# Hybrid decoder step on one core: the norm of k moved into the projection, tokens loaded and turned ahead, first weights rounded between modulated tiles

## What is computed

```python
m = silu(c) @ w_ada + b_ada             # shift1, scale1, gate1, shift2, scale2, gate2
h = x * (1 + scale1) + shift1
proj = h @ w_in                         # r, k, v, decay, a, gate columns, then q and kv latents and the rotary key
z = p_rwkv + mu * (shifted - p_rwkv)    # token shift; new_shift is the last row of p_rwkv
a = sigmoid(a0 + ad @ a2); g = sigmoid(gd) @ g2
kk = heads(k * k_k)
kk = kk / maximum(sqrt(sum(kk * kk, -1, keepdims=True)), 1e-12)
S, o = wkv_scan(S0, r, decay, k * (1 + (a - 1) * k_a), v, kk, a)
q = rmsnorm(cq, q_norm) @ w_q_up; lat = rmsnorm(ckv, kv_norm); kr = rope(kr, pos)
```

## Time and profile before

| | us |
|---|---|
| median of 3 runs | 2091.32 |
| lowest and highest run | 2089.89 and 2097.28 |
| profiled execution, its own time | 2096.06 |
| its span (first to last instruction) | 2094.3 |
| PE busy | 1862.8 (89%) |
| DVE busy | 1226.0 (59%) |
| POOL, ACT busy | 387.1, 381.1 (18% each) |

### The profile page before, as it was taken

One profiled execution on the slowest core, in us unless ns is written; L12 is line 12 of the kernel. 1 busy time (PEld: TensorE's weight loads), 2 busy tenths in 40 slices (PEclk: granted clock), 3 DMA queues, 4 the chain that ended last, 5 costly groups with the idle time before them and its releaser, 6 DMA issues.

```text
span 2094.3 us, 36235 instructions
## 1 busy us (share of the span) xinstructions
PE 1862.8 (89%) x14280; PEld 1637.6 (78%) x14280; DVE 1226.0 (59%) x1880; ACT 381.1 (18%) x809; POOL 387.1 (18%) x543
## 2 busy tenths in 40 slices
PE   5899996799999898773789599998999999989995
PEld 2688994577777665552579589998999999989995
DVE  1345854765666373230367777665766676657766
ACT  0433334223223232120210130000000000000002
POOL 0000102233333134523001341000100010001113
PEclk8899998899999896596999789999999999999997
DMA  9598521566666524105065325554555555545531
GB/s 350 192 333 311 168 86 48 167 213 215 209 217 196 182 76 119 49 20 183 1 201 161 121 83 167 170 166 141 161 161 161 158 166 162 161 128 169 168 100 45
DMA packets 300692, 329.08 MB, mean 157 GB/s; under 512 B 30419, under 2 KB 268532, under 8 KB 300084
## 3 DMA queue, kind: packets, MB, share of 16 engines
q1 hardware_dynamic: 291394, 314.83, 46.4%
q10 hardware_dynamic: 5548, 8.21, 1.2%
q0 software_dynamic: 3584, 3.68, 0.6%
HBM read 321.47 MB, written 5.21 MB: 156 GB/s over the span
## 4 chain that ended last, share of the span: by engine, by line
PE 82%; DVE 6%; DMA 5%; issue 3%; ACT 2%; SPq 1%; POOL 0%; ACTq 0%; DVEq 0%
PE bank L1347 15%; PE bank L1349 15%; PE bank L1348 15%; PE bank L1370 3%; DMA slab<-in_w_ada_dram 3%; PE bank L1371 3%; PE bank L1372 3%; PE bank L1484 3%; PE bank L1546 2%; PE bank L1556 2%; PE bank L1879 2%; PE bank L1554 1%; PE bank L1857 1%; PE bank L1332 1%; DVE xT L2505 1%
## 5 line engine op out<-in xcount | busy, mean ns | idle before, releaser
L1347 PE MATMUL bank<-arena_hi 128*128 128x288 f32 x2304 | 692.1, 300 | 32.9 <-DVE hT_lo L2049 19.7
L1349 PE MATMUL bank<-arena_hi,slab_lo 128*128 128x288 f32 x2304 | 684.6, 297 | 0.0
L1347 PEld LDWEIGHTS bank<-arena_hi 128*128 128x128 f32 x2304 | 438.1, 190 | 40.1 <-DVE hT_lo L2049 25.0
L1349 PEld LDWEIGHTS bank<-arena_hi,slab_lo 128*128 128x128 f32 x2304 | 440.8, 191 | 13.8 <-issue 13.8
L1348 PE MATMUL bank<-hT_lo,arena_hi 128*128 128x288 f32 x1280 | 384.8, 301 | 13.5 <-issue 13.5
L2445 DVE TENSOR_TENSOR slab_lo<-slab,arena_hi 128x2048 fp32r<-128x2048 f32 x144 | 352.1, 2445 | 5.0
L2444 DVE CAST arena_hi<-slab 128x2048 fp32r<-128x2048 f32 x144 | 176.8, 1228 | 302.3 <-PE bank L1349 294.9
L1348 PE MATMUL bank<-arena_hi 128*128 128x288 f32 x1024 | 302.1, 295 | 0.0
L1348 PEld LDWEIGHTS bank<-hT_lo,arena_hi 128*128 128x128 f32 x1280 | 247.5, 193 | 0.0
L1348 PEld LDWEIGHTS bank<-arena_hi 128*128 128x128 f32 x1024 | 192.2, 188 | 0.0
L878 POOL TENSOR_TENSOR arena<-arena 128x288 f32<-128x288 f32 x64 | 68.3, 1067 | 669.6 <-ACT arena L1275 669.6
(11 more groups left out here) (403 smaller groups left out, 2494.8 us busy)
## 6 DMA issues: line engine op xcount, KB each, us to landing
slab<-in_w_ada_dram SPq DMA_DIRECT2D x64, 1024.0 KB, 5.5
slab<-in_w_up_dram SPq DMA_DIRECT2D x32, 2048.0 KB, 8.8
slab<-in_w_down_dram SPq DMA_DIRECT2D x32, 2048.0 KB, 8.6
slab<-in_w_ada_dram SPq DMA_DIRECT2D x16, 2048.0 KB, 13.5
slab<-in_w_in_dram SPq DMA_DIRECT2D x15, 2048.0 KB, 11.4
slab<-in_w_out_dram SPq DMA_DIRECT2D x8, 2048.0 KB, 9.1
slab<-in_cache_latent_dram SPq DMA_DIRECT2D x96, 128.0 KB, 2.4
slab<-in_cache_latent_dram ACTq DMA_DIRECT2D x32, 128.0 KB, 3.5
```

The source lines that it names most:

```text
L1347: pe.matmul(b[0:w, 0:NTOK], w_hi[:, k, 0:w], x_hi[:, k, :], start=(k == 0), stop=False)
L1349: mm = pe.matmul(b[0:w, 0:NTOK], w_lo[:, k, 0:w], x_hi[:, k, :], start=False, stop=(k == KT - 1))
```

## The change

Three things.

- **Norm of k inside the projection.** While the projection runs, ACT squares k * k_k (parts 44 to 47 and 52 to 55), PE sums the squares of four tiles at a time into four 32-partition groups of one bank (`kk_sums`), ACT takes the square roots of two whole banks, and DVE takes maximum and reciprocal of both tiles in two instructions. In the LoRA loop a small product (`kk_spread`) spreads the two rows of a head tile over its 128 partitions, and DVE makes k * k_k * 1/norm in one instruction. POOL's products, the eight square roots and the eight reciprocals go. The last rows are turned by plain products into 32-partition groups of banks 4 and 5, after parts 57 and 59, copied by DVE between later weights and stored in 14 DMAs that SP issues ahead of the LoRA weights. tanh and sigmoid of the LoRA inputs move into the projection. The latents' norm and the key's rotation move to the four chunk steps of the last head tile. Some scratch tiles get other places.
- **Tokens ahead.** x is loaded by SP ahead of the first slabs. PE turns tokens 0 to 7 ahead of half 0, 8 to 11 ahead of half 1 and 12 to 15 behind turn 0, into four banks by turns.
- **First weights between modulated tiles.** ACT rounds the first weight part behind the first rounded tile, and DVE subtracts it behind that tile's low part.

The core of the diff:

```diff
 # SP
+            for q in range(2):
+                sp.dma_start(xrow[:, q, :], a["x_prompt"][0, q * P:(q + 1) * P, :]).then_inc(x_in, 16)
+            sp.dma_start(xrow[0:32, 2, :], a["x_sample"].rearrange("b t d -> (b t) d")).then_inc(x_in, 16)
             for m in range(4):
                 load_ada(m)
...
+            for c in range(7):
+                g, w = 32 * (c % 4), 512 if c < 6 else N_SHIFT - 6 * 512
+                cols = slice(512 * c, 512 * c + w)
+                sp.wait_ge(last_out, c + 1)
+                sp.dma_start(a["new_shift_prompt"][0, :, cols], last_four[g:g + 1, c // 4, 0:w]).then_inc(stored, 16)
+                sp.dma_start(a["new_shift_sample"][0][:, cols], last_four[g + 1:g + 9, c // 4, 0:w]).then_inc(stored, 16)
+
             s = LOR % RING
             wait_free(LOR)
...
-            sp.wait_ge(last_out, 7)
-            sp.dma_start(a["new_shift_prompt"], last_rows[0:1, 0, 0:N_SHIFT]).then_inc(stored, 16)
-            sp.dma_start(a["new_shift_sample"][0], last_rows[1:9, 0, 0:N_SHIFT]).then_inc(stored, 16)
 # POOL
-            for j in range(RT):
-                pool.wait_ge(win_mm, NWIN)
-                pool.tensor_scalar(hT[:, j, :], z[:, 8 + j, :], par[:, 128 + 16 + j:128 + 17 + j], None, ALU.mult).then_inc(kk_raw, 1)
...
-                pool.wait_ge(lora_sig, 2 * RT)
+                pool.wait_ge(lora_sig, 2 * j + 2)
...
-            pool.wait_ge(stored, 32)
+            pool.wait_ge(stored, 16 * 14)
+            pool.wait_ge(win_mm, NWIN)
+            pool.wait_ge(kk_mm, 2)
 # ACT
-            modulate_quarter(0)
+            act.wait_ge(mod_ready, 4)
+            act.wait_ge(x_ready, KT)
+            act.wait_ge(head_ready, 4)
             act.wait_ge(head_turned, 3)
-            for u in range(3):
+            modulate_prompt(0, 0, 16, 0)
+            modulate_prompt(0, 1, 16, 0)
+            high_part(0, 0, h_hi)
+            cast(0)
+            for k in range(2, 4):
+                modulate_prompt(0, k, 16, 0)
+                high_part(0, k - 1, h_hi)
+            high_part(0, 3, h_hi)
+            for u in range(1, 3):
                 cast(u)
...
             for u in range(30, U_MLA + 3):
                 cast(u)
+                if 44 <= u < 48:
+                    act.wait_ge(z_ready, 12)
+                    kk_square(u - 44)
+                if 52 <= u < 56:
+                    act.wait_ge(kk_mm, 1)
+                    kk_square(u - 48)
+            act.wait_ge(kk_mm, 2)
+            for b in range(2):
+                act.activation(rn[:, b, :], bank[6 + b][:, 0:NTOK], ACT.Sqrt).then_inc(kk_nrm, 1)
             for m in range(7):
+                if m == 2:
+                    act.wait_ge(z_ready, 4)
+                    act.activation(zl[0:LORA, 0, :], zl[0:LORA, 0, :], ACT.Tanh).then_inc(lora_turned, 1)
+                    act.activation(zl[:, 2:4, :], zl[:, 2:4, :], ACT.Sigmoid).then_inc(lora_turned, 1)
...
             for j in range(RT):
+                act.wait_ge(lora_mm, 2 * j + 1)
+                act.activation(sigw[:, j, :], bank[j % 2][:, 0:NTOK], ACT.Sigmoid, bias=par[:, P + j:P + j + 1]).then_inc(lora_sig, 1)
+                act.activation(ag[:, j, :], bank[2 + j % 2][:, 0:NTOK], ACT.Sigmoid, bias=par[:, P + 8 + j:P + 9 + j]).then_inc(lora_sig, 1)
                 if j == 0:
                     elementwise(0)
             for p in range(RT):
                 tiles(p)
             copy_d(RT - 1, 0)
             copy_states(RT - 1)
-            for c in range(1, NCH):
-                copy_d(RT - 1, c)
+            act.wait_ge(e_nt, 5 * RT)
+            act.wait_ge(win_kept, N_KEPT)
+            act.activation(sqm, mla[:, 0:4, :], ACT.Square).then_inc(m_sq, 1)
+            copy_d(RT - 1, 1)
+            act.wait_ge(m_mm, 1)
+            act.activation(sqm[:, 0:2, :], mla[:, 4:6, :], ACT.Square).then_inc(m_sq, 1)
+            copy_d(RT - 1, 2)
+            for n, dim in enumerate((QR, KVR)):
+                act.wait_ge(m_mm, n + 1)
+                act.activation(rin[:, n, :], bank[4 + n][:, 0:NTOK], ACT.Sqrt, scale=1.0 / dim, bias=eps[:, 1:2]).then_inc(m_std, 1)
+            copy_d(RT - 1, 3)
 # PE
-                pe.wait_ge(*((par_ready, 1) if k == 0 else (head_ready, 4) if k == 1 else (x_ready, k - 1)))
-                b = bank[6 + k % 2]
+                if k >= 4:
+                    pe.wait_ge(x_ready, k - 3)
+                b = bank[k % 4]
...
+            def kk_sums(b):
+
+                pe.wait_ge(kk_sq, 4 * b + 4)
+                for g in range(4):
+                    mm = pe.matmul(bank[6 + b][32 * g:32 * g + 32, 0:NTOK], blk[:, HD - 1:HD + 31], sq[:, g, :], start=True, stop=True)
+                mm.then_inc(kk_mm, 1)
+
+            def turn_last(chunks):
+
+                for e in range(4):
+                    for c in chunks:
+                        g, t = 32 * (c % 4), 4 * c + e
+                        w, at = (P, e * P) if t < 24 else (TILE_W[e], TILE_C[e])
+                        mm = pe.matmul(bank[4 + c // 4][g:g + 9, at:at + w], last[0:w, t, :], ident[0:w, 0:w], start=True, stop=True)
+                mm.then_inc(last_turned, len(chunks))
             for u in range(U_C, N_PARTS):
                 win_part(u, u == U_C)
+                if u == 47:
+                    kk_sums(0)
+                if u == 55:
+                    kk_sums(1)
+                if u == U_MLA + 1:
+                    pe.wait_ge(last_ready, 28)
+                    turn_last(range(4))
+                if u == U_MLA + 3:
+                    turn_last(range(4, 7))
+
+            def kk_spread(j):
+
+                g = 32 * (j % 4)
+                if j >= 2:
+                    pe.wait_ge(kk_ready, j - 1)
+                pe.matmul(bank[6 + j % 2][:, 0:NTOK], spread[g:g + 32, :], rn[g:g + 32, j // 4, :],
+                          start=True, stop=True).then_inc(kk_mm, 1)
...
             for j in range(RT):
                 if j >= 2:
                     wait(pe, lora_sig, 2 * j - 2)
                     wait(pe, g_ready, j - 1)
+                kk_spread(j)
...
                 chunk_o(RT - 1, c)
+                if c < 2:
+                    latent_sums(c)
+                if c == 2:
+                    pe.wait_ge(act_back, steps(AB_SNT, RT, AB_N))
+                    pe.matmul(SMP[0:64, 0:NTOK], rot, mla[0:64, 6, :], start=True, stop=True).then_inc(m_mm, 1)
             turn_prompt_state(RT - 1)
...
             pe.wait_ge(mod_ready, N_ADA + N_LATE)
+            pe.wait_ge(m_std, 2)
+            pe.wait_ge(kr_ready, 1)
 # DVE
             for u in range(U_MLA + 3, N_PARTS):
                 split(u)
...
+                if u == U_MLA + 3:
+                    dve.wait_ge(kk_nrm, 2)
+                    for h in range(2):
+                        dve.tensor_copy(spread[:, H[h]], const[:, C_SEL + h:C_SEL + h + 1].to_broadcast([P, HD]))
+                    ch.link(dve.tensor_scalar(rn, rn, 1e-12, None, ALU.max))
+                    dve.reciprocal(rn, rn).then_inc(kk_inv, 1)
+                if U_MLA + 5 <= u < U_MLA + 12:
+                    copy_last(u - (U_MLA + 5))
...
-                n = nrm[:, j % 2, :]
-                dve.wait_ge(kk_nrm, j + 1)
-                ch.link(dve.tensor_scalar(n, n, 1e-12, None, ALU.max))
-                ch.link(dve.reciprocal(n, n))
-                dve.wait_ge(kk_raw, j + 1)
-                dve.tensor_tensor(hT[:, j, :], hT[:, j, :], n, ALU.mult).then_inc(kk_ready, 1)
+                dve.wait_ge(kk_mm, 2 + j + 1)
+                dve.scalar_tensor_tensor(hT[:, j, :], z[:, 8 + j, :], par[:, P + 16 + j:P + 17 + j], bank[6 + j % 2][:, 0:NTOK],
+                                         ALU.mult, ALU.mult).then_inc(kk_ready, 1)
...
+            dve.wait_ge(z_ready, 28)
+            dve.wait_ge(stored, 16 * 14)
...
             for j in range(RT):
                 kk_norm(j)
+                dve.wait_ge(lora_mm, 2 * j + 2)
+                dve.tensor_copy(hT[:, 8 + j, :], bank[4 + j % 2][:, 0:NTOK]).then_inc(g_ready, 1)
+                if j == 0:
+                    scan(0)
+                if j == RT - 2:
                     elementwise(0)
...
             for c in range(NCH):
                 keep_u(RT - 1, c)
                 step_state(RT - 1, c)
+                if c == 2:
+                    dve.wait_ge(m_std, 1)
+                    ch.link(dve.reciprocal(rin[:, 0, :], rin[:, 0, :]))
+            latent_norm(0)
+            dve.wait_ge(m_std, 2)
+            ch.link(dve.reciprocal(rin[:, 1, :], rin[:, 1, :]))
+            latent_norm(1)
+            dve.wait_ge(m_mm, 3)
+            rotate(mla[0:64, 6, :], mla[0:64, 6, :], SMP[0:64, 0:NTOK], rot_m, kr_ready)
```

More of the change, by code:

```diff
@@ L892, in _ @@
             act.dma_start(const[:, :], a["const"]).then_inc(const_in, 16)
-            for q in range(2):
-                act.dma_start(xrow[:, q, :], a["x_prompt"][0, q * P:(q + 1) * P, :]).then_inc(x_in, 16)
```

(65 more changed lines are left out.)

85 lines of the change are left out of this document (21 added, 64 removed).

## The result

The changed kernel takes 2037.8 us (median of four runs, 2032.4 to 2041.1), the kernel before, run beside it, 2093.3 (four runs, 2089.9 to 2097.3). The profiled execution has a span of 2030.7 us, 63.6 less than that of before.

A forecast was written before the change was run, and what follows sets the result against it. TensorE was taken as the limit almost everywhere. −9.7 + 4.8 − 37.6 + 10.0 = −32.5 us takes the profiled 2096.06 to 2063.6, as a median 2059 us; range 2047 to 2074.

The forecast's parts named there:

- Part 1: At the head, tokens turned earlier and reordered first weights bring the first projection product 9.7 us earlier (ends −3.7, −13).
- rival A: At the head, x's 2.36 MB ahead in the queue delay every slab by 6.0 us: 2065 us, chance 0.10.
- The 1.9 of the first weights: At the head, the first weight rounding starts 1.4 us behind modulation's start, not 3.3: −1.9 us.
- Part 2: Inside the projection, PE's 8 sums of squares and 28 small products add 4.8 us (ends +3, +10).
- Rival B: Before the LoRA loop, queue order sends weights 6 to 8 us late; 2072 us with serial small products, chance 0.07.
- Part 3: Projection end to first inverse shrinks from 61.8 to 24.2 us, −37.6 (ends −41.5, −30).
- the added product: In the LoRA loop, each round gains one 288-column product of 0.48 us, going from 1.94 to 2.42.
- ACT's stall of 1.1: In the LoRA loop, round 3 waits for ACT's two sigmoids of round 1, losing 1.1 us.
- rival C: In the LoRA loop, ACT's exponentials hold up seven rounds by 3.4 us each: 2083 us, chance 0.06.
- The sum by the rows: In the LoRA loop, a table switch shows only 1.3 us; the skill's drain would add 2.8, making the total −29.7.
- Part 4: End of the recurrence: the latent norm in the last head tile's chunk steps adds 10.0 us (ends +5.7, +13).
- rival D: In the recurrence, removing the rest before it lowers the clock; at 14% low-clock time 2104 us, slower, chance 0.03.

## Why the prediction was wrong

**The step that failed is the sum**, which ended with the up-projections. All that follows was taken to move as a block, and some 20 us of it did not. The rows were there: 13.5 us of PE's waits in the loop had no releaser, three of them at one line, but the prediction reads no wait behind 740 us, because the change ends there. What decides them is the number of instructions ahead of a loop, which the change alters by 79 on TensorE. None of the rivals, nor the range, had room for it. That the shift made the loop shorter and not longer was luck: nothing in the change aimed at it. With the loop as it was, the median would have been near 2058 (2037.8 + 20.6, an estimate), which is inside the range.

Averaged over all profiles that have or lack a part:

| stretch | lacking it | having it | measured | forecast |
|---|---|---|---|---|
| head | 63.5 (3) | 48.7 (9) | −14.8 | −9.7 (−3.7 to −13) |
| projection | 258.4 (3) | 263.0 (9) | +4.6 | +4.8 (+3 to +10) |
| gap | 62.0 (3) | 26.5 (6) | −35.5 | −37.6 (−41.5 to −30) |
| tiles | 289.3 (3) | 290.6 (9) | +1.3 | 0 |
| end | 68.0 (3) | 76.0 (9) | +8.0 | +10.0 (+5.7 to +13) |
| loop | 880.8 (2, second wait at the old place) | 860.2 (5, no second wait) | −20.6 | 0 |
| sum | | | −57.0 | −32.5 |

In brackets stands the number of profiles; the gap leaves out those with the padded matrix, the loop those that are written out, and the two with 177 and 136 padding instructions. The medians differ by 55.5, so the account closes within 1.5 us. The stretches of the forecast alone come to −36.4.

- **Part 1**: the mechanism was right, the size was off. I had taken 0.85 a token and 1.81 a turn from rows at the low clock (0.66 from 28.5 to 39 us, 0.58 behind), for work that in the changed kernel comes behind 11.39 busy us in 11.50 and runs at the full one, 0.53 and 1.06; the far end of −13 named that, and the mean lies beyond it. In the one profile of after it is −12.9. Slabs 1 to 3 land at 28.3, 33.7 and 39.1, before at 28.5, 33.9 and 39.2: they do not come late, and rival A falls. (Slab 1's product starts at 30.3 and not at 28.5, because PE is still turning tokens.) PE now reaches slab 3 just after it lands (39.3), so still less work ahead of it would win next to nothing. The 1.9 of the first weights measured 1.94.
- **Part 2**: +4.6, and no new wait of PE or DVE at the projection's end; the weights' loop starts 0.7 behind it. Rival B falls. That +4.6 meets +4.8 is in part luck. Of the terms, the sums were put too low and the small products too high. PE's timeline of after has one group of each:

```profile
264.37 0.69 PE L1445 MATMUL bank<-arena,const 128*32 128x288 f32 x8
...
271.55 1.06 PE L1454 MATMUL bank<-const,arena 128*9 128x128 f32 x32
```

Both groups of sums take 1.4 where 1.1 was put down, and the 56 instructions of the small products 2.1 (1.06 and 1.05), where 3.8 was. Where the remaining 1 us lies stays open.

- **Part 3**: 26.5 instead of 24.2 (whose terms, added again, give 24.0). The term at fault is the added product, put at 0.48; it costs 0.88 (2.82 − 1.94), because 32 rows make it and its neighbour 0.20 slower each. Seven or eight such rounds are 2.8 to 3.2 more, and ACT's stall of 1.1, put into the sum, is hidden under the longer rounds: 1.7 to 2.1 net, of the 2.3 missing. Both showed when the matrix was padded. ACT stood in no round's way, so rival C falls.
- **Table switches**: ACT's timeline of after has a load in the loop, the pass ahead of it and the sigmoid right behind it:

```profile
318.66 0.21 ACT L1062 ACTIVATE arena<-arena 128x32 f32<-128x32 f32 x1
318.89 1.28 ACT L1147 ACT_TABLE_LOAD   x1
320.18 0.50 ACT L1147 ACTIVATE arena<-bank,par 128x288 f32<-128x288 f32 x1
```

The load starts 0.02 behind the pass and the sigmoid 1.29 behind the load's start. The drain of about 1.38 us that the Trainium skill adds ("ScalarE: Activation LUTs", section "What ACT_TABLE_LOAD costs") shows on neither side of it. The sum by the rows was the better one.

- **Part 4**: +8.0, each named step on the chain. It varied from 72.7 to 78.2 us between executions; what decides within that was not tried.
- **The prediction's rival D** falls: the recurrence keeps a clock of 1.00 (339 to 662 us). Where the tiles' +1.3 comes from stays open.

## What to carry to other kernels

In a loop that an engine runs with a jump, read the waits for "issue" at its first lines: they can depend on how many instructions stand ahead of it, so any change upstream may win or lose them, and the loop's time then says little about the change. Before a result is believed, cut both spans at the same places; where a stretch moved that the change doesn't touch, shift its code by idle instructions, or write the loop out. A forecast that stops where the change stops should say what it takes for granted behind it.

## What the hardware showed

- The second wait after a jump back cost up to 5.9 us with 19 or 20 instructions to the next border, up to 3.8 with 60, nothing with 195 or 196; the first one was there in every kernel with a jump, up to 2.0. The second waits end 1.2 to 1.5 us behind the landing of a 16 KB packet of code, and the borders lie 256 instructions apart. Why a packet comes so late was not isolated: in the one case shown it started 6.7 us after the one before had landed, and the DMA engines were full with weights for the last 4.8 of these. VectorE's waits at its own jumps were longer, up to 8.1 us.
- Between products on more rows, a product on 32 of 128 rows took 0.68 instead of 0.48 us, and the next one also 0.68.
- The granted clock of one and the same stretch came out at 0.56 in one execution and 0.84 in another of the same code; the stretch took 139.9 and 130.4 us.
